# TensorE's expert kinds and the head of their loop moved to multiples of 256 instructions

## What is computed

```python
def swiglu(h, w_gate, w_up, w_down):
    return (jax.nn.silu(h @ w_gate) * (h @ w_up)) @ w_down

def moe_swiglu(h, router_w, router_b, w_gate, w_up, w_down):
    logits = jnp.einsum('bsd,de->bse', h, router_w) + router_b
    top_vals, top_idx = lax.top_k(logits, TOP_K)          # TOP_K = 2
    top_w = jax.nn.softmax(top_vals, axis=-1)
    combine = jnp.sum(jax.nn.one_hot(top_idx, N_EXPERTS) * top_w[..., None], axis=-2)
    y = jnp.zeros_like(h)
    for e in range(N_EXPERTS):                             # 8 experts, hidden width 3584
        y = y + combine[..., e:e + 1] * swiglu(h, w_gate[e], w_up[e], w_down[e])
    return y
```

## Time and profile before

| | |
|---|---|
| median of the timed runs | 2431.33 us |
| profiled execution, its own time | 2433.15 us |
| its span in the trace | 2431.3 us |
| TensorE busy | 2379.6 us, 98% of the span |
| VectorE busy | 861.8 us |
| ScalarE busy | 357.6 us |
| mean granted TensorE clock | 0.998 of full speed |
| the loop over the experts | about 1472 to 2424 us |

### The profile page before, as it was taken

The page is one execution under the profiler, slowest core; times in us unless marked ns, Lnnn a source line. Parts: engine busy times, 40 slices in busy tenths (PEclk is TensorE's granted clock), DMA queues, the critical chain, the costliest instruction groups (busy, mean ns, idle before and its releaser), DMA issues.

```text
span 2431.3 us, 28995 instructions
## 1 busy us (share of the span) xinstructions
PE 2379.6 (98%) x11570; PEld 1574.2 (65%) x11571; DVE 861.8 (35%) x1820; ACT 357.6 (15%) x961; POOL 54.9 (2%) x110
## 2 busy tenths in 40 slices
PE   9999999999999999999999999989999989999998
PEld 8956476679665666676777756548995544445444
DVE  4565242255563367663344462201002101011101
ACT  2254010012351100101000111101001101010101
POOL 0000000000000000000000000000000000000000
PEclk9999999999999999999999999999999999999999
DMA  7422343444322778435576469999669999779970
GB/s 278 147 109 96 112 173 139 174 152 178 115 105 75 289 277 334 196 145 229 223 287 281 166 253 392 425 426 427 251 252 372 425 426 425 317 313 426 427 286 36
DMA packets 78978, 617.42 MB, mean 254 GB/s; under 512 B 5984, under 2 KB 6112, under 8 KB 39184
## 3 DMA queue, kind: packets, MB, share of 16 engines
q1 hardware_dynamic: 73920, 558.39, 57.7%
q0 software_dynamic: 4656, 56.47, 5.7%
q10 hardware_dynamic: 288, 0.90, 0.1%
HBM read 614.69 MB, written 1.05 MB: 253 GB/s over the span
## 4 chain that ended last, share of the span: by engine, by line
PE 90%; DMA 6%; DVE 2%; ACT 1%; issue 1%; SPq 0%; DVEq 0%; POOL 0%; POOLq 0%; ACTq 0%
PE T L2450 9%; PE S L2803 8%; PE S L2801 8%; PE G L2189 6%; DMA big<-in_moe_pack 5%; PE G L2466 5%; PE G L2817 4%; PE G L2815 4%; PE G L2221 3%; PE G L2404 3%; PE S L2680 3%; PE T L2680 3%; PE G L2703 3%; PE S L2867 2%; PE G L2532 2%; PE G L2416 2%
## 5 line engine op out<-in xcount | busy, mean ns | idle before, releaser
L2801 PE MATMUL S<-big,hT 128*64 128x256 f32 x2240 | 270.0, 383 | 21.7 <-DMA big<-in_moe_pack 19.6
L2044 DVE TENSOR_TENSOR turns<-S,turns 128x128 f32<-128x128 f32 (+2 forms) x105 | 35.5, 338 | 672.8 <-ACT turns L1217 672.8
L2801 PEld LDWEIGHTS S<-big,hT 128*64 128x64 f32 x2240 | 156.8, 137 | 130.6 <-issue 49.2
L2450 PE MATMUL T<-hT,big 128*128 128x256 f32 x960 | 217.1, 379 | 1.1 <-ACT big L1122 1.1
L2450 PEld LDWEIGHTS T<-hT,big 128*128 128x128 f32 x960 | 182.1, 190 | 49.5 <-issue 27.7
L2803 PE MATMUL S<-big,hT 128*128 128x512 f32 x448 | 201.7, 593 | 3.0 <-issue 2.9
L2803 PEld LDWEIGHTS S<-big,hT 128*128 128x128 f32 x448 | 82.8, 190 | 97.8 <-issue 97.8
L2221 PE MATMUL G<-big,hT 128*128 128x384 f32 x320 | 109.0, 490 | 0.8 <-ACT big L1012 0.8
L1222 ACT ACTIVATE pT<-T 128x128 f32<-128x128 f32 (+1 forms) x98 | 30.1, 308 | 530.0 <-PE T L2780 530.0
L2189 PE MATMUL G<-big 128*128 128x186 f32 (+1 forms) x536 | 91.7, 322 | 0.0
L2189 PEld LDWEIGHTS G<-big 128*128 128x128 f32 x536 | 86.6, 190 | 0.2
(11 more groups left out here) (456 smaller groups left out, 3271.8 us busy)
## 6 DMA issues: line engine op xcount, KB each, us to landing
big<-in_moe_pack SPq DMA_DIRECT2D x112, 2048.0 KB, 15.9
big<-in_moe_pack SPq DMA_DIRECT2D x72, 1024.0 KB, 14.0
big<-in_w_ff SPq DMA_DIRECT2D x32, 2048.0 KB, 8.8
big<-in_ada_pack POOLq DMA_DIRECT2D x24, 2048.0 KB, 12.0
big<-in_ffn_pack SPq DMA_DIRECT2D x11, 3072.0 KB, 13.4
big<-in_gate_pack SPq DMA_DIRECT2D x16, 1536.0 KB, 6.5
consts<-in_moe_pack SPq DMA_DIRECT2D x24, 1024.0 KB, 14.5
big<-in_proj_pack SPq DMA_DIRECT2D x15, 1488.0 KB, 6.5
```

The costliest lines, as they stand in the source:

```text
L2450: ins = mm(up_bank(c, f), w[:, k, f * P:(f + 1) * P], hT[:, k, :], start=(k == 0), stop=(k == KD - 1))
L2801: ins = mm(S[s % 2][f * FEW:(f + 1) * FEW, 0:SEQ], hTe[:, k, 0:FEW], wt[:, k, f * SEQ:(f + 1) * SEQ], start=(k == 0), stop=(k == KD - 1))
```

## The change

```diff
             turn = nc.alloc_registers(f"{name}_turn", engines=[eng.engine])
             nc.regs_mov(turn, 0)
+            if begin:
+                eng.addr_align(256, 0, 3)
             eng.br(f"{name}_head")
...
                     eng.br_lt(turn, EXPERTS, on_true=f"{name}_head", on_false=f"{name}_done{w}").branch_hint(again)
                     with nc.body(f"{name}_done{w}", valid_engines=[eng.engine]):
+                        if begin:
+                            eng.addr_align(256, 255, 3)
                         eng.br(f"{name}_end")
```

## The result

The changed kernel takes 2443.97 us, median of 5 executions (2443.18 to 2448.26), against 2432.33 us before (5 executions, 2428.73 to 2435.28). The ratio is 1.005, 95% interval 1.0039 to 1.0061: slower by 0.5%, 11.6 us, where 10.2 were forecast. The profiled execution is the longest of its five (2448.26 us, span 2446.5), so its trace shows some 4 us more than the median does.

What follows compares the result with a forecast made beforehand. TensorE, busy 98% of the span, was taken as the bound. Full kind's gaps +8.8, clock +3.5, few kind's stops -1.3 and -0.8 gave +10.2 us on the 2431.33 median: 2441.5 us, 8-in-10 range 2430 to 2447.

Steps and rivals of the forecast that it cites:

- the map: Slot positions of head and kinds in 256-instruction code blocks, counted from the code and from stops after 15 and 9 matmuls.
- few kind's two stops: Few kind's first products, turns 3 and 6: waits for the next code block go, -0.80 and -1.30 us.
- The 0.8 us of turn 3: Few kind's stop in turn 3: gain taken in full; low bound 0 if turn 4's weight waits eat it.
- The full kind's first block: Branch to the full kind, turns 5 and 7: block not fetched, 6.3 us for 0.35; +4.4 us each, +8.8 together.
- The reading behind it: Few kind's last block: the next block isn't fetched during the tail, since the head is hinted next.
- The clock term: Behind each gap ahead of the full kind: slow clock costs 1.76 us, bounds 0 and 3.5; +3.5 together.
- the forecast's own range: 2437 us (no clock loss, turn 3 gain whole) to 2446 us (clock cost doubled), around 2441.5.
- The costs put at 0: Loop entry over padding (0 to +1 us), wide kind's back edge and the `done` padding, each taken as 0.
- The back edge into turn 3: Wide kind's tail: the head will be found there, the 6.32 us go, but lay beside scatter matmuls: 0.
- A: Full kind's start: the block behind is fetched after all and the 5.0 us of stops vanish; 2426.4 us, chance 0.12.
- B: No telling difference: padding not placed as asked, or the branch's fetch half as long; 2431.6 us, chance 0.10.
- C: Only eight newest blocks held, so one more miss, up to 6.3 us in turn 6; 2444 to 2452 us, chance 0.08.

Runs made afterwards that it cites:

- experiment 1: The changed kernel without the few kind's hint, at its start and on its back edge; 2428.37 us, ratio 0.9981 to the kernel before.
- experiment 5: The kernel before, with no directive, without the few kind's hint; 2429.37 us, ratio 0.9986 to the kernel before.
- experiment 3: The changed kernel without the first directive: only the kinds aligned, the head left at slot 67; 2444.79 us, ratio 1.0046 to the kernel before.
- experiment 7: The changed kernel run again unaltered; 2447.04 us, ratio 1.0052 to the kernel before.
- experiment 4: The changed kernel with the full kind at slot 200 of the few kind's last block, head at slot 0; 2429.1 us, ratio 0.9984 to the kernel before.
- experiment 2: The changed kernel without the second directive, so only the head is aligned; 2434.54 us, ratio 1.0005 to the kernel before.
- experiment 6: The changed kernel without the hints of the few and the full kind; 2436.06 us, ratio 1.0016 to the kernel before.

## Why the prediction was right

**The stops and the map.** That the few kind's two stops would go was right in turn 6. It gave 1.7 us, not 1.3: besides the stop itself, the 15 and 17 matmuls around it take 1.94 and 2.16 us, 4.10 together, against 3.67 for 32 in one run.

**The 0.8 us of turn 3** were taken in full and came to nothing. Turns 3 and 4 together take 0.3 us more than before. The weights set the end of turn 4: there the changed kernel waits 10.8 us for them and the one before 9.3 (first row after, second before, both in the stretch of turn 4):

```profile
PE S L2805 <- DMA big<-in_moe_pack: 10.8, 7, 1.9
```

```profile
PE S L2801 <- DMA big<-in_moe_pack: 9.3, 7, 1.7
```

The low bound, 0, was the one that held: TensorE starts sooner and waits longer.

**The full kind's first block** was the step that decided, and it held: from the branch to the first product 6.9 and 6.6 us were measured (2024.0 to 2030.92 and 2273.6 to 2280.19), 6.8 forecast. The reading behind it, that the hint keeps the next block out, was only argued ahead of the result, from packets that weren't there. Experiments 1 and 5 show it: they differ from their partners by the hint alone, and the packet and the short branch come with its absence.

**The clock term** was mis-sized: 1.76 us forecast for each gap, 2.7 and 2.6 measured in the first trace (9.79 and 9.75 us against 7.13), 2.1 to 2.8 over the six such gaps of this kernel and experiments 3 and 7. The estimate came from a gap of 2.1 us and the stretch of slow clock behind it; a gap of 6 us left a stretch of slow clock twice as long, most of it behind the gap. It lay inside the bounds of 0 and 3.5. Corrected for this, for turn 3 and for turn 6 the sum is 10.2 + 2 x 0.9 + 0.8 - 0.4 = 12.4, and the medians say 11.6 in the first comparison and 14.3 in experiment 7. The ends of the forecast's own range are also 1 us wider than its terms give: 2431.3 + 6.7 is 2438.0, not 2437, and 2431.3 + 13.7 is 2445.0, not 2446.

**The costs put at 0.** The back edge into turn 3 fell from 6.32 to 0.38 us and gave nothing, as it lay beside the scatter products. The branch over the padding ahead of the head does wait for its block: 0.86 and 2.17 us lie open ahead of turn 0 in experiments 4 and 2. In experiment 2 turn 1 ends no later for it; in experiment 4 it ends 1.6 us later than in the kernel before, so whether the wait for weights takes such a stop back stays open. In the profiled execution of the changed kernel slower gather products cover it (6.12 us for the 24 that take 4.88 before); in the second trace of this kernel 0.23 us lie open.

**The rivals.** A, that the next block is fetched after all, is what happens without the hint, and its number, 2426.4 us, is near what experiment 1 gave, 2428.37. B fell with the branch's 6.4 and 6.0 us. C didn't come in the changed kernel, whose back edge into turn 6 takes 0.37 us. A miss there is what experiment 2 shows for another place of the full kind. The condition that C rests on, that the eight newest blocks are held, doesn't fit the changed kernel's packets (experiment 6): it keeps the head over nine fetches.

The Trainium skill ("Runtime: NRT & Kernel Launch", Instruction fetch mechanics) calls the prefetch purely sequential. The trace agrees in a kind without a hint (the packet from 1908 to 1920 us in experiment 1) and differs in the last block of a kind that holds a hinted back edge (none from 1905 to 2023 us in the changed kernel).

## What to carry to other kernels

In a loop with several bodies, ask of each jump which block of code its target lies in, and who has run or asked for that block before. A round number at a body's start moves it away from what its neighbour has just fetched; a start inside the neighbour's last block, with enough work left ahead of the next border, is better. A prefetch hint isn't free: it takes the place of the fetch in sequence. The few kind, which with the head stays held in six blocks, did better here without one. The full kind did better with it, provided that it ended well inside a block. Some 3 us of the kernel before can be had by leaving one hint out (experiment 5).

## What the runs showed of the hardware

A jump to a block of code that isn't held costs 6.0 to 6.6 us in nine cases seen here with the weights streaming (5.0 in a tenth, into turn 3 of experiment 5), though the packet itself is short: one packet takes 13.5% of 16 engines over half a microsecond, 1.1 us, and in the nine cases it starts 3.4 to 4.1 us after the jump.

A hinted fetch seems to be made only when the block with the hinted branch is entered, however early the hint stands. The back edge into turn 6 takes longer the fewer slots of that block the full kind fills (slots from the map in the prediction; the packet of the head against the start of the back edge):

| kernel | slots in the last block | packet of the head | back edge, us |
|---|---|---|---|
| experiment 1 | 103 | 6.6 us ahead | 0.48 |
| before | 80 | 7.0 us ahead | 0.48 |
| experiment 4 | 47 | 0.9 us ahead | 1.63 |
| experiment 2 | 13 | 4.1 us behind | 6.62 |
| experiment 6, no hint | 102 | 3.9 us behind | 6.34 |
| changed | 103 | none in turn 5 | 0.37 |

The last row is another case: the head wasn't fetched again there at all, and its short back edge says nothing of the hint.

A gap of some 6 us on TensorE costs 2.1 to 2.8 us more behind it, by a clock at half speed, and the gaps of 4.5 and 4.8 us of experiments 6 and 2 cost 2.3 us (32 matmuls in 6.01 and 6.02 us against 3.67); a gap of 1.35 us cost nothing of that kind.
